# A hybrid decoder layer with expert retrieval: the second phase's work spread over 282 gather steps instead of 255, and row copies in halves through the bank of picks

## The reference, cut to what matters

```python
q = (hb @ w_peer_q).reshape(PEER_BLOCK, PEER_HEADS, 2, PEER_HALF)
s = jnp.einsum('thpc,hpkc->thpk', q, sub_keys, preferred_element_type=F32)
...
u_rows = jnp.take(expert_u, idx, axis=0)
a = jnp.einsum('td,tkd->tk', hb, u_rows, preferred_element_type=F32)
wgt = (g * jax.nn.gelu(a, approximate=False)).astype(hb.dtype)
v_rows = jnp.take(expert_v, idx, axis=0)
return jnp.einsum('tk,tkd->td', wgt, v_rows)
```

## Time and profile before

| | |
|---|---|
| runs of the kernel before | 2157.54, 2160.86 and 2162.66 us (median 2160.86) |
| the profiled execution | 2159.08 us |
| its span | 2157.3 us |
| PE busy / clock granted over the span | 75% / 0.829 |
| DVE, ACT, POOL busy | 64%, 38%, 37% |
| mean traffic of the DMA engines | 345 GB/s |

### The profile page before, as it was taken

One profiled execution on the slowest core, in us unless ns is written; L12 is line 12 of the kernel. 1 busy time (PEld: TensorE's weight loads), 2 busy tenths in 40 slices (PEclk: granted clock), 3 DMA queues, 4 the chain that ended last, 5 costly groups with the idle time before them and its releaser, 6 DMA issues.

```text
span 2157.3 us, 33388 instructions
## 1 busy us (share of the span) xinstructions
PE 1607.8 (75%) x11692; PEld 733.1 (34%) x11692; DVE 1373.2 (64%) x3347; ACT 826.9 (38%) x2404; POOL 788.6 (37%) x713
## 2 busy tenths in 40 slices
PE   7989999898998898778887998895444445444444
PEld 3556655444444444434443433341110001100000
DVE  2577665113458677876776666347777767777774
ACT  2122323202545444544546543334433333433332
POOL 1254200001323244433443332334455555455553
PEclk9999999999999999988899999998655556555555
DMA  5333456837999899999999999999999999999998
GB/s 190 145 115 115 173 202 254 311 137 237 381 418 372 347 367 413 372 374 362 375 385 411 399 412 412 380 418 406 421 419 422 420 411 412 419 417 414 421 410 346
DMA packets 125794, 745.14 MB, mean 345 GB/s; under 512 B 15892, under 2 KB 39052, under 8 KB 47916
## 3 DMA queue, kind: packets, MB, share of 16 engines
q0 software_dynamic: 78336, 570.46, 65.3%
q1 hardware_dynamic: 47292, 172.55, 21.4%
HBM read 727.36 MB, written 16.44 MB: 345 GB/s over the span
## 4 chain that ended last, share of the span: by engine, by line
PE 38%; DMA 28%; DVE 20%; issue 7%; ACT 4%; POOL 2%; SPq 0%; DVEq 0%; POOLq 0%; ACTq 0%
DMA ring<-in_expert_uv,pick 27%; PE z L1182 22%; DVE ring L1962 7%; PE acc L1354 5%; PE z L1188 2%; PE o L1217 1%; ACT fold L1527 1%; DVE ti L1845 1%; DVE ti L1848 1%; PE s L1207 1%; DVE tmp L2033 1%; POOL ring L1114 1%; DVE tv L1847 1%; POOL ssq L1080 1%; PE o L1305 1%
## 5 line engine op out<-in xcount | busy, mean ns | idle before, releaser
L1114 POOL DMA_INDIRECT ring<-in_expert_uv,pick x544 | 657.5, 1209 | 878.4 <-PE acc L1354 812.6
L1962 DVE CUSTOM_DVE_ANT_0 ring<-ring,rep 128x1024 f32<-128x1024 f32 x544 | 664.6, 1226 | 403.3 <-DMA ring<-in_expert_uv,pick 360.1
L1354 PE MATMUL acc<-ring,fold 128*32 128x256 f32 x4352 | 457.4, 506 | 454.3 <-ACT fold L1527 453.6
L1182 PE MATMUL z<-wts,hT 128*128 128x384 f32 (+1 forms) x1408 | 604.5, 567 | 3.0 <-ACT hT L1573 2.6
L1354 PEld LDWEIGHTS acc<-ring,fold 128*32 128x32 f32 x4352 | 104.3, 125 | 778.4 <-ACT fold L1527 714.8
L1524 ACT ACTIVATE gel<-dots 128x1 f32<-128x1 f32 x544 | 108.8, 200 | 616.6 <-DVE dots L1962 615.9
L1182 PEld LDWEIGHTS z<-wts,hT 128*128 128x128 f32 x1408 | 259.0, 198 | 252.0 <-issue 187.3
L1182 PE MATMUL z<-wts,yT 128*128 128x512 f32 x384 | 185.8, 619 | 4.0 <-ACT yT L1723 1.8
L1527 ACT ACTIVATE fold<-by_pick,gel 128x32 f32<-128x32 f32 x544 | 174.8, 321 | 18.1 <-ACT gel L1524 0.2
L1520 ACT ACTIVATE by_pick<-cst,pick 128x32 f32<-128x32 f32 x544 | 167.3, 308 | 0.0
L1837 DVE SCALAR_TENSOR_TENSOR yT<-uT,vec,yT 128x256 f32<-128x256 f32 x240 | 107.2, 501 | 2.0
(11 more groups left out here) (256 smaller groups left out, 1617.5 us busy)
## 6 DMA issues: line engine op xcount, KB each, us to landing
wts<-in_w_qkv SPq DMA_DIRECT2D x24, 1536.0 KB, 9.0
wts<-in_w_glu SPq DMA_DIRECT2D x8, 2048.0 KB, 13.1
wts<-in_w_gate SPq DMA_DIRECT2D x8, 2048.0 KB, 12.4
wts<-in_w_wq SPq DMA_DIRECT2D x8, 2048.0 KB, 10.8
ring<-in_k_cache SPq DMA_DIRECT2D x16, 768.0 KB, 7.7
ring<-in_v_cache SPq DMA_DIRECT2D x16, 768.0 KB, 7.9
ring<-in_expert_uv,pick POOLq DMA_INDIRECT x544, 11.6
wts<-in_w_cp SPq DMA_DIRECT2D x4, 2048.0 KB, 11.0
```

The lines of the kernel that those rows point to most:

```text
L1114: eng.indirect_dma_start(ring[:, i % RING, :], None, a["expert_uv"], bass.IndirectOffsetOnAxis(picks(i, 0).bitcast(U32), 0)).then_inc(row_ ...
L1182: mm = eng.matmul(bank[:, 0:w], of[:, k, :], rows[:, k, :], start=(k == 0), stop=(k == depth - 1))
L1354: mm = eng.matmul(acc[b][SUB * c:SUB * (c + 1), col:col + 256], fold[:, i % 4, :], ring[:, i % RING, D + 256 * c:D + 256 * (c + 1)], start ...
L1962: eng.tensor_tensor_reduce(u, u, rep[:, j, :], 1.0, 0.0, ALU.mult, ALU.add, dots[:, i % 4:i % 4 + 1]).then_inc(dot_ready, 1)
```

## The change

`step_marks` now reaches `hi` = 272 at the tick after the one that scores tile 2's first two heads (tick 476) and goes on at the same slope, so that the last tick ends at mark 299. The search at step 272 needs only those scores. All marks of phase two rise with it, by a tenth. The copies of tile 2 then fall beside the last query projections, whose banks `zb` are in use. So `copy_rows` writes one half at a time into `ob`, the bank of picks, and is called twice for each group, two steps apart (276, 278, ... 290 for tile 2; 404, 406, ... 418 for tile 3). It waits for the eviction of the half before and for `place` of the last picks; `spread` waits for the eviction of the last half. ACT evicts a half two steps after PE's step (`LEAD_A + 1`), and `rep_ready` counts halves. The picks whose `spread` falls within the ticks move with the marks: those of tile 2's heads 0 and 1 are now spread in ticks 484 and 498.

```diff
@@ copies_made
-        out.setdefault(max(slot_before(t, j) + 4, BASE[2] - LAG + 4 + 2 * n), []).append((n, t, j))
+        at = max(slot_before(t, j) + 1, BASE[2] - LAG + 4 + 4 * n)
+        for q in range(2):
+            out.setdefault(at + 2 * q, []).append((2 * n + q, t, j, q))
...
-MADE_NO = {(t, j): n for some in MADE.values() for n, t, j in some}
+MADE_NO = {(t, j): n for some in MADE.values() for n, t, j, q in some if q}
@@ step_marks
+    kept = next(n for n, some in enumerate(TICKS) if ("SC", 2, 0) in some) + 1
     for n in range(ENDS[0], len(TICKS)):
-        marks[n] = lo + int((hi - lo) * rest[n - ENDS[0]] / rest[-1] + 1e-9)
+        marks[n] = lo + int((hi - lo) * rest[n - ENDS[0]] / rest[kept - ENDS[0]] + 1e-9)
@@ PE
+            copied, spreads = [0], [0]
+
             def spread(q):
 
                 bank_free(eng, OB, [o_free, o_free], ("P", q))
+                if copied[0]:
+                    eng.wait_ge(rep_ready, copied[0])
+                spreads[0] = OB.no["P", q] + 1
                 eng.wait_ge(ig_ready, q + 1)
...
-            def copy_rows(n, t, j):
+            def copy_rows(n, t, j, q):
 
                 if n:
                     eng.wait_ge(rep_ready, n)
-                else:
-                    eng.wait_ge(h2_ready, NTH["N1", 3] + 1)
-                    for u in USES[-2:]:
-                        freed(eng, ZB, z_free, u)
-                for q in range(2):
-                    for c in range(QUAD):
-                        mm = eng.matmul(zb[q][SUB * c:SUB * (c + 1), :], own_rows(j), h2s[:, t % 2, 512 * q:512 * (q + 1)], start=True, stop=True)
+                if q == 0:
+                    eng.wait_ge(h2_ready, NTH["N1", t] + 1)
+                eng.wait_ge(o_free, max(o_phase(1), spreads[0]))
+                for c in range(QUAD):
+                    mm = eng.matmul(ob[SUB * c:SUB * (c + 1), :], own_rows(j), h2s[:, t % 2, 512 * q:512 * (q + 1)], start=True, stop=True)
                 mm.then_inc(rep_made, 1)
+                copied[0] = n + 1
@@ ACT
-                    for n, u, k in MADE.get(i, ()):
+                    for n, u, k, w in MADE.get(i - LEAD_A - 1, ()):
                         eng.wait_ge(rep_made, n + 1)
-                        eng.wait_ge(dot_ready, slot_before(u, k) + 1)
-                        for w in range(2):
-                            ins = eng.activation(rep[:, k, 512 * w:512 * (w + 1)], zb[w][:, :], ACT.Copy)
-                        ins.then_inc(rep_ready, 1)
+                        if w == 0:
+                            eng.wait_ge(dot_ready, slot_before(u, k) + 1)
+                        eng.activation(rep[:, k, 512 * w:512 * (w + 1)], ob[:, :], ACT.Copy).then_inc(rep_ready, 1)
```

## The result

The kernel after takes 2165.52 us, the kernel before 2158.85 us (medians of 20 runs each). The ratio is 1.0031, interval [1.0021, 1.0042]: **6.7 us slower** (4.5 to 9.1), where 7 us faster was forecast. The profiled execution has a span of 2164.1 us, 6.8 us more than before.

What follows compares the result with a forecast made beforehand. The DMA engines were taken as the closer limit of the second phase, with PE near, and as the pace of the tail. -68.4 + 61.5 = -7 us gave 2154.0 us, range 2139 to 2171 us.

Steps and rivals of the forecast that it cites:

- The marks move 27 steps, -68.4 us in the tail.: Tail: 27 steps move into the second phase, each saving 2.53 us of tail, -68.4 us.
- PE, VectorE and DMA prices: Second phase: 27 more steps cost PE 17.6 us, VectorE 50 us and the DMA engines 70.5 us.
- The copies of rows: Tile 2's four copies beside the last query projections: about 8 us of PE, hidden in its idle time, cost nothing.
- The 9 us of spare that would be filled: Second phase: of 27 us spare DMA time, 9 is filled, so the phase grows by 70.5 - 9 = 61.5 us.
- the first rival: Second phase: DMA engines simply full, none of the spare 27 us filled; +2 us, 2163 us; chance 24%.
- the three stretches: 720 to 750, 870 to 880 and 1060 to 1090 us: 18 us of spare DMA time, taken to stay unfilled.
- The new waits on the bank of picks: Steps 408 and mark 280: PE held until picks are taken, 0 to 5 us each, taken as 0.
- The rival in which VectorE becomes the pace and the kernel gets slower: Attention part: POOL's 14 waits for VectorE's sums lengthen; +10 us at half, 2171 us, up to 19 slower; chance 20%.
- PE paces the whole phase: Second phase: only PE's 17.6 us and the copies' 8 are paid; -43 us, 2118 us; chance 3%.
- all spare filled: Second phase: a deeper backlog of gathers fills every spare DMA moment; -25 us, 2136 us; chance 8%.
- The signs to look for: Profile after: phase end about 1526 us, wrong before 1515 or after 1535; DMA share 0.99; folded-gate wait beyond 75 us.

Runs made afterwards that it cites:

- the copies alone: The changed kernel with the old marks, ending at 272, so half copies through the bank of picks all fall in the tail: 2157.87 us, ratio 0.9992.
- thin-load kernels: Kernel before and changed kernel, each with phase-two weight loads cut to 256 columns per partition: 2116.45 us (ratio 0.9815) and 2104.66 us (ratio 0.9756).

## Why the prediction was wrong, point by point

- *The marks move 27 steps, -68.4 us in the tail.* Right: what follows the phase is 70.5 us shorter, and a step in the tail takes 2.55 us.
- *PE, VectorE and DMA prices.* PE's 0.65 us per step holds (188.29 / 290). For a gather the queue's row of the kernel after gives 0.787 x 966 / 290 = 2.62 us, against 2.61 taken. Of the 40 slices I read two things too smoothly, which bears on no term: PE is at 7 tenths in four of the first 26, and the DMA digit is below 9 in the first ten. The queues' rows of the kernel after:

```profile
q0 software_dynamic: 41672, 303.38, 78.7%
q1 hardware_dynamic: 20084, 71.37, 18.8%
```

- *The copies of rows: "I cost them at nothing: PE's 127 idle us ... hide them."* **This is the step that failed most.** The forecast missed by 13.7 us, and 7.6 of them are here: without the copies the change costs nothing (-0.9 us), with them +6.7 us, without PE's products +0.6 us. The 127 us were PE's idle time over 890 us. The end of the phase has little of it: PE was busy 36.90 of the last 40 us before, and 39.58 of the 40 us after in which five of the copies start. I had the 8 us ready as "no such cover", and the cover was indeed missing.
- *The 9 us of spare that would be filled.* **This term failed too,** for the other 6 us of the miss. Without copies the 27 steps are worth -0.9 us (interval -3.7 to +1.9), against my -7 and the first rival's +2, which is the nearer. The phase of that kernel leaves (1.01 - 0.98) x 956 = 29 us unused, as much as before:

```profile
575.00:1531.00 956.00, 800.16 (x5658) 371.66 (x5656) 651.34 (x1597) 444.86 (x1242) 371.65 (x328) 0.93 0.98 393
```

That the three stretches keep their idle time was only partly so. In the kernel after the one at the convolution is smaller (0.92 from 735 to 765 us, 2.7 us lost), and one of 3 us stands ahead of it, where POOL waits 9.1 us for PE. The one at 870 to 880 us now stands at 890 to 930 us, with POOL's waits of 5.8 and 5.9 us for VectorE's sums in it:

```profile
700.00:715.00 15.00, 12.80 (x116) 5.89 (x116) 13.59 (x41) 7.69 (x22) 4.72 (x4) 0.89 0.80 309
890.00:930.00 40.00, 29.08 (x175) 16.19 (x175) 34.69 (x100) 18.24 (x55) 15.73 (x14) 0.83 0.83 320
```

- *The new waits on the bank of picks, taken at 0.* Right in the tail: the copies alone cost -1.7 us, and doubled products at tile 3 add nothing. Beside the projections a half copy waits up to 1.3 us for the eviction of the half before, and a small part of the 7.6 us may be in that.
- *The rival in which VectorE becomes the pace and the kernel gets slower.* It named the right side and the wrong mechanism. POOL's wait for the sums is as it was, 56.2 us in 12 waits against 54.2 in 14, and it did not lengthen 14 times by 0.5 us. Waits of the kernel after from 575 to 1545 us:

```profile
POOL ring L1117 <- PE acc L1361: 507.2, 210, 10.6
...
DVE ring L1968 <- DMA ring<-in_expert_uv,pick: 211.6, 111, 7.6
...
PE acc L1361 <- ACT fold L1534: 95.5, 74, 5.6
POOL ssq L1082 <- DVE ssq L2023: 56.2, 12, 8.2
```

- *PE paces the whole phase; all spare filled.* Neither came. The Trainium skill's ceiling of 435 GB/s ("DMA: Bandwidth & Descriptors", section "Where 436 GB/s comes from") would have given all 27 gathers room. The trace does not agree: the phase moves 389 GB/s before and after, although 40 us of it reach 421.
- *The signs to look for.* PE's wait for folded gates did grow beyond 75 us, to 95.5. The DMA share was to rise to 0.99 and stayed at 0.98. The phase's end beyond 1535 us was named as a sign against me, and came (1541.0), but with POOL's sums as the place to look. The right place was the DMA share of the last 40 us.

What stays open: why marks to 286, with five half copies still beside the projections, pay nothing for them (-2.4 us; the interval reaches +0.4, so it may be nothing); how much of the price is in the evictions; and which waits keep the thin-load kernels from gaining more.

## What to carry to other kernels

Idle time of an engine averaged over a phase is no cover for work that lands in one place of it: cut the window where the work will stand, and see whether the resource that paces the kernel still has its supply there. When work is moved towards a phase that already keeps the pacing resource full, what it can bring is that resource's idle time and no more, and here it did not bring even that; what moves along with it (here eight half copies) has to be priced at the place where it lands. A move in small doses in both directions shows quickly whether a kernel already stands on the flat part of the curve: here 27 steps fewer cost 13 us, while 14 more with the copies, and 27 more without them, changed nothing that could be measured.

## What the runs showed of the hardware

The DMA share did not measure an amount of work that stays the same. The gathers of the second phase carry 274 MB in the kernel before and 275 MB with thin weights, but with weights beside them their packets take 0.772 x 890 = 687 us, and with thin weights 0.845 x 848 = 717 us:

```profile
q0 software_dynamic: 37757, 274.96, 84.5%
q1 hardware_dynamic: 19781, 20.44, 7.5%
```

Here the same queue moved the same bytes in less busy time when the other queue had more to do (71 MB against 20), and a share of 0.92 went with only 350 GB/s. I had not expected that; a share near 1 tells less of how much fits beside it than the bytes and an experiment do.
